# A fused two-block transformer kernel: overlapping row steps with the last attention units, and narrowing the pooling products

## The chip, the cores and the metric

The kernel runs on one core of a Trainium2 chip. The metric is the time of one execution on the device in microseconds (us). Three runs of the kernel before took 3562.31, 3562.95 and 3566.51 us; the median is 3562.95 us.

## The reference

Everything is in fp32. A first block runs twice (layers 0 and 1) over 256 tokens of `x` and 256 tokens of `ctx`, each 2048 wide; a second block (retention, recurrence, cross attention, feed-forward) follows once and is not touched. What concerns us in a layer:

```
p  = h @ w_in[l]                       # pool values, pool gate, q, k, v, attention gate
q, k = rope(rms_norm(q)), rope(rms_norm(k))    # per 64-wide half head; ctx rows have no rope
# 8 heads, each of two 64-wide halves:
a  = softmax(q0 @ k0.T) - lam * softmax(q1 @ k1.T)
o  = rms_norm(a @ v)                   # per head of 128
pooled = windowed mean over tokens (2, 4, 8 or 16 wide) - v   # four groups of 256 columns
x  = x + gate * (concat(mix(pooled) * silu(pool gate), o * silu(attention gate)) @ w_out[l])
```

In layer 0 the queries of both `x` and `ctx` are served (x queries see all 512 keys, ctx queries the 256 of ctx); in layer 1 only those of `x`. The windowed mean is a product with a constant 256 x 256 matrix per window size, which is zero away from a band round its diagonal: no token looks further than 8 tokens back or ahead.

## The kernel before

**Products.** Every large product streams its weights in pieces of 256 rows by 512 columns. ScalarE rounds a piece to `w_hi` (`split_hi`), VectorE makes the remainder `w_lo` (`split_lo`), and TensorE adds three fp32r products, hi by hi, lo by hi and hi by lo, for two groups of 128 rows and each token tile of 128 (`piece_pe`, L617 on). A piece is thus 24 matmuls for four token tiles and 12 for two. `w_hi` and `w_lo` are rings of four; the splits are made three pieces ahead (`AHEAD`). A chunk is eight pieces. At its end ScalarE copies the result to `stage` (`store_act`) and POOL's queue stores it to DRAM (`store_pool`). For four tiles ScalarE takes those copies in the chunk's last piece, ahead of whatever else is woven in there, and so is held until that piece ends.

**What is woven in.** Each engine has its own instruction stream, written as a generator of steps. `together` runs the pieces of a list of products and, after each piece, takes as many steps of the woven generator as the rate says (`advance`). With a rate of 1.125 every eighth piece is followed by two steps; with 1.25 every fourth; with 0.75 three steps fall on four pieces. All engines use the same rates, so step s stands after the same piece on each of them. Nothing but semaphores ties them together: VectorE and ScalarE may run up to three pieces ahead of TensorE.

**The attention stage.** In each layer it is woven into 64 pieces (`beside0`, `beside1`). In layer 0 all have four token tiles; in layer 1 the first 16 pieces have four and the other 48 have two. The stage handles four heads at a time (a group, `attn[l][hg]`, hg = 0, 1). A group has, in this order:

- 2 empty steps (time for loads);
- 7 row steps. Four tiles of q and k rows, numbered k, are normalised and turned. For tiles 0 and 1 one step squares (ScalarE), sums (VectorE), takes the root (ScalarE) and scales (VectorE); a second applies rope (six VectorE instructions, L1060 to L1064). Tiles 2 and 3 have one step each. TensorE transposes the tiles (L1115) in row steps 2, 4, 5 and 6, and ScalarE copies the results to `qT`, `kT`;
- 16 units in layer 0 and 8 in layer 1, plus 2 draining steps. In step s TensorE makes the scores of unit s (L1130), transposes the probabilities of unit s - 1 (L1138) and multiplies those of unit s - 2 with v (L1146). Between them VectorE takes the maximum (L1073), ScalarE the exponential (L1002), VectorE the combination (L1084), ScalarE the copies (L1010, L1016);
- closings, 2 in layer 0 and 1 in layer 1: the rms norm of the results (square L1023, sum L1089, root L1025, scale L1093) and their store to `o1`.

After group 1 comes `close_*`, 14 steps in layer 0 and 20 in layer 1: pooling (`pooling_pe`), mixing, gating, turning. In all that is 29 + 29 + 14 = 72 steps in layer 0 (rate 1.125) and 20 + 20 + 20 = 60 in layer 1 (rate 1.25 for 16 pieces, 0.75 for 32, 1.0 for 16).

`rt` holds the squares of even row tiles and of the closings; `e_sb[:, 0]` those of odd row tiles; both halves of `e_sb` hold exponentials of units. Row tile 2 is loaded into `aT`, which the units also use.

**Pooling.** For each of 8 column blocks `pooling_pe` adds two fp32 products over the 256 output tokens: one over source tokens 0 to 127 and one over 128 to 255. It runs three times in the kernel: x and ctx of layer 0, x of layer 1. A full fp32 matmul stands as two records in the trace.

Of the kernel before, what the change touches and what calls it, by code (L numbers as in the profile page):

```python
# [9 lines left out]
ALU = mybir.AluOpType  # L10
ACT = mybir.ActivationFunctionType
AX = mybir.AxisListType

P = 128
# [63 lines left out]
def build_program(nc, t, out):  # L78
    ctx = ExitStack()
    with ctx:  # L80
# [834 lines left out]

        inv_q = small[:, 160:192]
        squares = [rt, e_sb[:, 0].rearrange("p x c -> p (x c)")]

        def group_pool(pool, gr, l, hg, rows_ready, v_ready, following):
# [6 lines left out]
            for tt in range(4):  # L926
                pool.dma_start(v_sb[:, tt, :], p1[tt, :, O_V + 512 * hg:O_V + 512 * hg + 512]).then_inc(v_loaded, 16)
            yield
            yield
            slots, turned = slots_of(gr)  # L930
            for n in range(len(slots) + 1):
                if turned.get(n) == 0:
                    load_qk(pool, gr, hg, 3)
                yield
            for s in range(len(gr["units"]) + 2):
                if following and s == len(gr["units"]) - 2:
                    wait_all(pool, following[1])
                    load_qk(pool, following[0], hg + 1, 0)
                    load_qk(pool, following[0], hg + 1, 1)
                if not following and s == 1:  # L940

                    pool.wait_ge(qk_T, 2 * gr["m0"] + 8)
                    pool.dma_start(poolA[:], t["pool_a"]).then_inc(pl_a_loaded, 16)
                yield
            if not following:

                pool.wait_ge(o_ready, gr["n0"] + len(gr["units"]))
                wait_all(pool, stored_by(plan[f"beside{l}"][-5]))
                pooling_pool(pool, 2 * l, l, [0, 1])
                pool_weights(pool, l)  # L950
            for c in range(gr["closings"]):
                pool.wait_ge(on_done, gr["c0"] + c + 1)
                for tt in (2 * c, 2 * c + 1):
                    pool.dma_start(o1[tt, :, 512 * hg:512 * hg + 512], o_tok[:, tt, :]).then_inc(o_stored, 16)
                yield

        def group_act(act, gr):
            yield
            yield
# [58 lines left out]
            for c in range(gr["closings"]):  # L1018
                act.wait_ge(o_copied, gr["n0"] + len(units))
                if gr["c0"] + c:  # L1020
                    act.wait_ge(on_ssq, gr["c0"] + c)
                act.wait_ge(qk_done, gr["m0"] + 4)
                nc.scalar.activation(rt[:], o_tok[:, 2 * c:2 * c + 2, :].rearrange("p t c -> p (t c)"), ACT.Square).then_inc(on_sq, 1)  # L1023
                act.wait_ge(on_ssq, gr["c0"] + c + 1)
                nc.scalar.activation(small[:, 136:144], small[:, 128:136], ACT.Sqrt, bias=eps_col[:], scale=1.0 / P).then_inc(on_rms, 1)  # L1025
                yield

        def group_dve(dve, link, gr):
            yield
            yield  # L1030
            slots, turned = slots_of(gr)
            for s in range(len(slots) + 1):
                if s < len(slots):
# [52 lines left out]
                yield  # L1086
            for c in range(gr["closings"]):
                dve.wait_ge(on_sq, gr["c0"] + c + 1)
                nc.vector.tensor_reduce(small[:, 128:136], rt[:].rearrange("p (h c) -> p h c", c=P), AX.X, ALU.add).then_inc(on_ssq, 1)  # L1089
# [4 lines left out]
                yield  # L1094

        def group_pe(pe, gr):
            yield
            yield
# [1413 lines left out]
        for l in range(DEPTH):  # L2512
            groups = []
            for hg in range(2):
                preps = [(tt, l == 0 or tt < XT) for tt in range(4)]
                units_ = [(h, qt, 0 if qt < XT else 2, 4 if qt < XT else 2) for h in range(4) for qt in range(4 if l == 0 else 2)]
                gr = dict(ada=(10, 12)[l], preps=preps, units=units_, m0=m, n0=n, c0=c0, closings=2 if l == 0 else 1, loads=[], evacs=[])
# [11 lines left out]
                groups.append(gr)  # L2529
            attn.append(groups)  # L2530

        def attention_pool(pool, l):
            for hg, gr in enumerate(attn[l]):
                first = plan["lanes0"][2] if l == 0 else plan["lanes1"][1]
                beside = plan[f"beside{l}"]
                rows_ready = [(ada_used, KT * (10, 12)[l])] + stored_by(first)
                following = None if hg else (attn[l][1], stored_by(beside[1 - l]))
                steps = group_pool(pool, gr, l, hg, rows_ready, stored_by(beside[l]) if hg else [], following)
                for n, _ in enumerate(steps):
                    if hg == 0 and n == 1:  # L2540
                        gate_rows_pool(pool, l)
                    if hg == 0 and n == 11:
                        gate_keep_pool(pool, l)
                    yield
            yield from close_pool(pool, l)

        def attention_act(act, l):
            for gr in attn[l]:
                yield from group_act(act, gr)
            yield from close_act(act, l)  # L2550

        def attention_dve(dve, link, l):
            for hg, gr in enumerate(attn[l]):
                for n, _ in enumerate(group_dve(dve, link, gr)):
                    if hg == 0 and n == 10:
                        gate_rows_dve(dve, link, l)
                    yield
            yield from close_dve(dve, link, l)

        def attention_pe(pe, l):  # L2560
            for gr in attn[l]:
                yield from group_pe(pe, gr)
            yield from close_pe(pe, l)

        ATTN_RATE = [1.125, [1.25] * 2 + [0.75] * 4 + [1.0] * 2]

        block = ctx.enter_context(nc.Block())

# [356 lines left out]
```

## Time and profile before

| what | value |
|---|---|
| runs | 3562.31, 3562.95, 3566.51 us |
| the profiled execution | 3565.26 us |
| its span in the trace | 3563.6 us |
| TensorE busy | 3495.1 us (98%), granted clock 0.996 on average |
| VectorE, ScalarE, POOL busy | 1893.7, 1650.5, 220.2 us |
| attention stage of layer 0 | about 476 to 935 us of the span |
| attention stage of layer 1 | about 1296 to 1560 us |

The profiled execution is 1.7 us longer than its span. TensorE is busy nearly always, but a busy TensorE isn't one at its peak: its clock can be granted at half, and a record's end is modelled. The rows further down say where it waits and what it waits for. A granted clock of 1.00 is 2.4 GHz and 0.50 is 1.2 GHz.

### The profile page before, as it was taken

Reading aid. Unit: us, or ns where it says so; the run is one execution under the profiler, and the core shown is the slowest. Engines: PE = TensorE matmul, PEld = TensorE weight load, DVE = VectorE, ACT = ScalarE, POOL = GpSimd, SP = SyncE. Lnnn points to the kernel's source line nnn. Section 1 sums busy time; section 2 is a strip of 40 time slices with the busy share of each in tenths; the row PEclk is TensorE's granted clock in tenths of the full one; section 3 lists DMA queues with packets and bytes.
Section 4 is the critical chain, followed back from the end, with each engine's and each line's share of the span. In section 5 each row is a group of like instructions: output and inputs, shape, how many; then the busy total and the mean of one; then the engine's idle time right before and its main releaser. Section 6 shows DMA issues by size and latency. Waiting matters only on the chain.

```text
span 3563.6 us, 45550 instructions
## 1 busy us (share of the span) xinstructions
PE 3495.1 (98%) x17098; PEld 2820.0 (79%) x17098; DVE 1893.7 (53%) x2345; ACT 1650.5 (46%) x2157; POOL 220.2 (6%) x409
## 2 busy tenths in 40 slices
PE   7999999999999999999999999999999999999998
PEld 5777777777888777688888888888888888888887
DVE  3361134543477335656547775566644566666544
ACT  5441234444345234544545654444454466666433
POOL 2010010101000011000010000000000000000000
PEclk9999999999999999999999999999999999999999
DMA  9979952424566753576777667676654666666665
GB/s 361 345 265 352 331 169 94 142 89 152 194 210 210 242 192 132 172 234 186 217 241 227 212 212 261 204 239 189 208 171 149 188 185 186 183 186 185 201 194 160
DMA packets 331250, 736.85 MB, mean 207 GB/s; under 512 B 26359, under 2 KB 26961, under 8 KB 327872
## 3 DMA queue, kind: packets, MB, share of 16 engines
q1 hardware_dynamic: 300224, 627.12, 55.3%
q0 software_dynamic: 30704, 106.24, 8.4%
q8 instruction: 119, 1.95, 0.2%
q10 hardware_dynamic: 144, 1.05, 0.1%
q14 instruction: 59, 0.48, 0.0%
HBM read 689.10 MB, written 45.21 MB: 206 GB/s over the span
## 4 chain that ended last, share of the span: by engine, by line
PE 93%; DVE 4%; ACT 2%; DMA 1%; issue 1%; POOL 0%; ACTq 0%; SPq 0%; DVEq 0%; POOLq 0%
PE psum L624 28%; PE psum L626 27%; PE psum L625 27%; PE psum L493 2%; DVE w_lo L526 1%; PE psum L1130 1%; PE psum L1146 1%; ACT w_hi L518 1%; PE psum L1173 1%; PE psum L1188 1%; PE psum L2306 1%; PE psum L1138 1%; PE psum L1948 0%; PE psum L686 0%; PE psum L2103 0%
## 5 line engine op out<-in xcount | busy, mean ns | idle before, releaser
L526 DVE TENSOR_TENSOR w_lo<-w_raw,w_hi 128x1024 fp32r<-128x1024 f32 x997 | 1218.6, 1224 | 1424.4 <-ACT w_hi L518 1421.9
L518 ACT ACTIVATE w_hi<-w_raw 128x1024 fp32r<-128x1024 f32 x997 | 1052.9, 1059 | 1369.6 <-PE psum L626 1307.4
L624 PE MATMUL psum<-w_hi,a_hi 128*128 128x512 f32 x3072 | 1219.3, 397 | 4.5 <-DVE a_lo L1230 1.9
L626 PE MATMUL psum<-w_hi,a_lo 128*128 128x512 f32 x3072 | 1198.4, 390 | 0.0
L625 PE MATMUL psum<-w_lo,a_hi 128*128 128x512 f32 x3072 | 1197.2, 390 | 0.0
L624 PEld LDWEIGHTS psum<-w_hi,a_hi 128*128 128x128 f32 x3072 | 578.0, 188 | 137.2 <-issue 12.6
L626 PEld LDWEIGHTS psum<-w_hi,a_lo 128*128 128x128 f32 x3072 | 577.4, 188 | 122.5
L625 PEld LDWEIGHTS psum<-w_lo,a_hi 128*128 128x128 f32 x3072 | 578.3, 188 | 115.3
L624 PE MATMUL psum<-w_hi,f_hi 128*128 128x512 f32 x704 | 276.0, 392 | 0.0
L626 PE MATMUL psum<-w_hi,f_lo 128*128 128x512 f32 x704 | 274.2, 390 | 0.0
L625 PE MATMUL psum<-w_lo,f_hi 128*128 128x512 f32 x704 | 273.9, 389 | 0.0
L562 POOL DMA_DIRECT2D p<-stage x152 | 83.1, 548 | 1465.2 <-ACT stage L554 760.2
L626 PEld LDWEIGHTS psum<-w_hi,f_lo 128*128 128x128 f32 x704 | 132.2, 188 | 27.8
L625 PEld LDWEIGHTS psum<-w_lo,f_hi 128*128 128x128 f32 x704 | 132.3, 188 | 26.7
L624 PEld LDWEIGHTS psum<-w_hi,f_hi 128*128 128x128 f32 x704 | 132.2, 188 | 26.7
L1002 ACT ACTIVATE e_sb<-psum,small 128x512 f32<-128x512 f32 (+1 forms) x96 | 67.0, 702 | 181.3 <-DVE small L1074 181.2
L624 PE MATMUL psum<-w_hi,g_hi 128*128 128x512 f32 x352 | 137.1, 390 | 0.0
L626 PE MATMUL psum<-w_hi,g_lo 128*128 128x512 f32 x352 | 137.0, 389 | 0.0
L625 PE MATMUL psum<-w_lo,g_hi 128*128 128x512 f32 x352 | 136.9, 389 | 0.0
L624 PE MATMUL psum<-w_hi,mem_hi 128*128 128x512 f32 x256 | 102.7, 401 | 3.0 <-DVE mem_lo L2616 3.0
L625 PE MATMUL psum<-w_lo,mem_hi 128*128 128x512 f32 x256 | 100.5, 393 | 0.0
L626 PE MATMUL psum<-w_hi,mem_lo 128*128 128x512 f32 x256 | 100.5, 392 | 0.0
(384 smaller groups left out, 2783.7 us busy)
## 6 DMA issues: line engine op xcount, KB each, us to landing
w_raw<-w_in SPq DMA_DIRECT2D x416, 512.0 KB, 4.3
ada_raw<-w_ada SPq DMA_DIRECT2D x192, 512.0 KB, 7.1
w_raw<-ffn_w_up SPq DMA_DIRECT2D x176, 512.0 KB, 3.7
w_raw<-w_out SPq DMA_DIRECT2D x96, 512.0 KB, 4.7
w_raw<-ffn_w_down SPq DMA_DIRECT2D x88, 512.0 KB, 4.7
p<-stage POOLq DMA_DIRECT2D x152, 256.0 KB, 4.5
w_raw<-xa_w_k SPq DMA_DIRECT2D x32, 512.0 KB, 8.9
w_raw<-xa_w_v SPq DMA_DIRECT2D x32, 512.0 KB, 6.3
```

The source lines that it names most:

```text
L493: mm = nc.tensor.matmul(psum[32 * j:32 * j + 2, ADA_BANK[u % 2], 0:256], cond_st[:, kt, :], ada_raw[ada_home[a]][:, j, :], start=kt == 0, ...
L518: nc.scalar.activation(w_hi[:, slot], raw_of(k), ACT.Copy).then_inc(hi_ready, 1)
L526: nc.vector.tensor_tensor(w_lo[:, slot], raw_of(k), w_hi[:, slot].bitcast(F32), ALU.subtract).then_inc(lo_ready, 1)
L562: pool.dma_start(g.more["to"](tt, g.col(i, c, g.body)), stage_of(g, c, tt)).then_inc(stored[bank], 16)
L624: nc.tensor.matmul(acc, g.hi[:, tt, kt, :], w_hi[:, slot, kk, :], start=first, stop=False)
L625: nc.tensor.matmul(acc, g.hi[:, tt, kt, :], w_lo[:, slot, kk, :], start=False, stop=False)
L626: mm = nc.tensor.matmul(acc, g.lo[:, tt, kt, :], w_hi[:, slot, kk, :], start=False, stop=last)
L1002: nc.scalar.activation(e_sb[:, n % 2, x, 0:nk * P], psum[:, 4 + x, 0:nk * P], ACT.Exp, bias=small[:, sm + x:sm + x + 1], scale=inv_q[:, 8 ...
L1130: nc.tensor.matmul(psum[:, 4 + x, 0:nk * P], qT[64 * x:64 * x + 64, h, qt * P:(qt + 1) * P], kT[64 * x:64 * x + 64, h, k0 * P:(k0 + nk) * ...
L1138: mm = nc.tensor.transpose(psum[:, 6, b * P:(b + 1) * P], a_sb[:, (n - 1) % 2, b * P:(b + 1) * P], ident[:])
L1146: mm = nc.tensor.matmul(psum[:, 7, 0:P], aT[:, n % 2, b * P:(b + 1) * P], v_sb[:, k0 + b, h * P:(h + 1) * P], start=b == 0, stop=b == nk - 1)
L1173: mm = nc.tensor.matmul(psum[:, b, 256 * (cc % 2):256 * (cc % 2) + 256], pv[:, m, cc * P:(cc + 1) * P], poolA[:, cc // 2, m, :], start=m = ...
```

## The change

Four things change together.

1. The steps of a layer are laid out by `staggered`. The second group has no empty steps, and starts when the first has its two draining steps and its closings still before it, so that in those steps both parts are executed, the first's part ahead of the second's on each engine. `close_*` likewise starts with the second group's closings. Layer 0 now has 64 steps (second group from step 25, close from step 50) and layer 1 has 54 (17 and 34).
2. The rates become 1.0 in layer 0, and 1.0, 0.6875 and 1.0 in layer 1.
3. Buffers and loads are adapted: the closings square into `e_sb[:, 1]` (with two added waits on ScalarE), the second group's tiles 0 and 1 are loaded two unit steps earlier, its tile 2 and its v move to the row step in which tile 3 was loaded already.
4. The pooling product over source tokens 128 to 255 is made for output tokens 120 to 255 alone (136 columns in place of 256).

```diff
         def group_pool(pool, gr, l, hg, rows_ready, v_ready, following):
+            def values():
+                wait_all(pool, v_ready)
+                for tt in range(4):
+                    pool.dma_start(v_sb[:, tt, :], p1[tt, :, O_V + 512 * hg:O_V + 512 * hg + 512]).then_inc(v_loaded, 16)
+
             if hg == 0:
                 wait_all(pool, rows_ready)
-                load_qk(pool, gr, hg, 0)
-                load_qk(pool, gr, hg, 1)
-            load_qk(pool, gr, hg, 2)
-            wait_all(pool, v_ready)
...
-            yield
-            yield
+                for k in range(3):
+                    load_qk(pool, gr, hg, k)
+                values()
+            for _ in range(gr["idle"]):
+                yield
             slots, turned = slots_of(gr)
             for n in range(len(slots) + 1):
                 if turned.get(n) == 0:
+                    if hg:
+                        load_qk(pool, gr, hg, 2)
                     load_qk(pool, gr, hg, 3)
+                    if hg:
+                        values()
                 yield
             for s in range(len(gr["units"]) + 2):
-                if following and s == len(gr["units"]) - 2:
+                if following and s == len(gr["units"]) - 4:
...
         def group_act(act, gr):
...
+                    if s == 1 and gr["c0"]:
+                        act.wait_ge(on_ssq, gr["c0"])
...
-                act.wait_ge(qk_done, gr["m0"] + 4)
-                nc.scalar.activation(rt[:], o_tok[:, 2 * c:2 * c + 2, :].rearrange("p t c -> p (t c)"), ACT.Square).then_inc(on_sq, 1)
+                act.wait_ge(a_ready, gr["n0"] + len(units))
+                nc.scalar.activation(o_squares, o_tok[:, 2 * c:2 * c + 2, :].rearrange("p t c -> p (t c)"), ACT.Square).then_inc(on_sq, 1)
...
         def pooling_pe(pe, s):
...
-                for m in range(XT):
-                    mm = nc.tensor.matmul(psum[:, b, 256 * (cc % 2):256 * (cc % 2) + 256], pv[:, m, cc * P:(cc + 1) * P],
-                                          poolA[:, cc // 2, m, :], start=m == 0, stop=m == XT - 1)
+                for m, first in ((0, 0), (1, P - 8)):
+                    mm = nc.tensor.matmul(psum[:, b, 256 * (cc % 2) + first:256 * (cc % 2) + 256], pv[:, m, cc * P:(cc + 1) * P],
+                                          poolA[:, cc // 2, m, first:], start=m == 0, stop=m == XT - 1)
...
+        def staggered(l, first, second, closing):
+
+            units = len(attn[l][0]["units"])
+            second_at = attn[l][0]["idle"] + 7 + units
+            going = [(0, first), (second_at, second), (second_at + 7 + units + 2, closing)]
+            step = 0
+            while going:
+                for part in list(going):
+                    if part[0] <= step:
+                        try:
+                            next(part[1])
+                        except StopIteration:
+                            going.remove(part)
+                step += 1
+                if going:
+                    yield
...
-        ATTN_RATE = [1.125, [1.25] * 2 + [0.75] * 4 + [1.0] * 2]
+        ATTN_RATE = [1.0, [1.0] * 2 + [0.6875] * 4 + [1.0] * 2]
```

## Rows read from the trace of the kernel before

**Rows 1.** The page: the chain that ended last, by engine.

```profile
PE 93%; DVE 4%; ACT 2%; DMA 1%; issue 1%; POOL 0%; ACTq 0%; SPq 0%; DVEq 0%; POOLq 0%
```

**Rows 2.** Waits of TensorE, layer 0's stage (480 to 930): total us, times, longest.

```profile
PE psum L1130 <- ACT e_sb L1002: 5.6, 3, 2.5
PE psum L1115 <- DVE qk L1054: 4.9, 1, 4.9
PE psum L1115 <- DVE qk L1064: 1.4, 1, 1.4
PE psum L1138 <- DVE a_sb L1084: 0.8, 2, 0.5
PE psum L1146 <- ACT o_tok L1016: 0.6, 1, 0.6
```

**Rows 3.** Stretches of TensorE: length, busy us (instructions), granted clock, DMA share, GB/s.

```profile
530.00:535.00 5.00, 5.00 (x17) 0.67 0.21 52
...
760.00:765.00 5.00, 4.65 (x19) 0.50 0.00 0
...
825.00:830.00 5.00, 3.27 (x15) 0.68 0.45 177
...
1365.00:1370.00 5.00, 3.27 (x21) 1.00 0.35 105
```

**Rows 4.** The chain that ended last, in order of time: start, us, what.

```profile
527.80 1.97 PE psum L1115 x8
...
552.06 0.89 PE psum L1146 x8
...
761.75 1.71 PE psum L1146 x8
...
874.79 6.91 PE psum L1173 x32
```

**Rows 5.** Waits of TensorE, layer 1, the sixteen four-tile pieces (1296 to 1401).

```profile
PE psum L1130 <- ACT e_sb L1002: 1.7, 1, 1.7
PE psum L1115 <- DVE qk L1064: 1.0, 1, 1.0
PE psum L1130 <- ACT kT L989: 0.7, 1, 0.7
PE psum L1138 <- DVE a_sb L1084: 0.4, 1, 0.4
```

**Rows 6.** Waits of TensorE, layer 1, the two-tile pieces (1401 to 1500).

```profile
PE psum L1138 <- DVE a_sb L1084: 2.7, 5, 1.1
PE psum L1115 <- DVE qk L1064: 2.0, 2, 1.4
PE psum L1115 <- DVE aT L1054: 1.1, 1, 1.1
PE psum L1130 <- ACT e_sb L1002: 1.0, 2, 0.7
PE psum L1115 <- DVE qk L1054: 0.7, 1, 0.7
```

**Rows 7.** VectorE's timeline, layer 0, group 0's closing, then group 1's first row tile.

```profile
655.56 1.21 DVE L1089 TENSOR_REDUCE small<-rt 128x8 f32<-128x1024 f32 x1
...
657.38 1.22 DVE L1093 TENSOR_TENSOR o_tok<-o_tok,small 128x1024 f32<-128x1024 f32 x1
...
676.09 1.23 DVE L526 TENSOR_TENSOR w_lo<-w_raw,w_hi 128x1024 fp32r<-128x1024 f32 x1 [4.21 <-ACT w_hi L518]
677.24 1.21 DVE L1044 TENSOR_REDUCE small<-rt 128x16 f32<-128x1024 f32 x1
...
679.31 0.69 DVE L1052 TENSOR_TENSOR qk<-qk,small 128x512 f32<-128x512 f32 x1
...
682.75 1.43 DVE L1060 TENSOR_TENSOR rt<-qk,rope_s 128x256 f32<-128x256 f32 x4
...
685.47 1.23 DVE L1064 TENSOR_TENSOR qk<-qk,rt 128x1024 f32<-128x1024 f32 x1
```

More of the change, by code:

```diff
@@ L917, in build_program @@
         squares = [rt, e_sb[:, 0].rearrange("p x c -> p (x c)")]
+        o_squares = e_sb[:, 1].rearrange("p x c -> p (x c)")
         def group_pool(pool, gr, l, hg, rows_ready, v_ready, following):
+            def values():
+                wait_all(pool, v_ready)
+                for tt in range(4):
+                    pool.dma_start(v_sb[:, tt, :], p1[tt, :, O_V + 512 * hg:O_V + 512 * hg + 512]).then_inc(v_loaded, 16)
             if hg == 0:
                 wait_all(pool, rows_ready)
-                load_qk(pool, gr, hg, 0)
-                load_qk(pool, gr, hg, 1)
-            load_qk(pool, gr, hg, 2)
-            wait_all(pool, v_ready)
-            for tt in range(4):
-                pool.dma_start(v_sb[:, tt, :], p1[tt, :, O_V + 512 * hg:O_V + 512 * hg + 512]).then_inc(v_loaded, 16)
-            yield
-            yield
+                for k in range(3):
[3 more added lines that the diff above has]
+                yield
             slots, turned = slots_of(gr)
@@ L957, in group_act @@
         def group_act(act, gr):
-            yield
-            yield
+            for _ in range(gr["idle"]):
+                yield
             slots, turned = slots_of(gr)
@@ L1028, in group_dve @@
         def group_dve(dve, link, gr):
-            yield
-            yield
+            for _ in range(gr["idle"]):
+                yield
             slots, turned = slots_of(gr)
@@ L1088, in group_dve @@
                 dve.wait_ge(on_sq, gr["c0"] + c + 1)
-                nc.vector.tensor_reduce(small[:, 128:136], rt[:].rearrange("p (h c) -> p h c", c=P), AX.X, ALU.add).then_inc(on_ssq, 1)
+                nc.vector.tensor_reduce(small[:, 128:136], o_squares.rearrange("p (h c) -> p h c", c=P), AX.X, ALU.add).then_inc(on_ssq, 1)
                 dve.wait_ge(on_rms, gr["c0"] + c + 1)
@@ L1096, in group_pe @@
         def group_pe(pe, gr):
-            yield
-            yield
+            for _ in range(gr["idle"]):
+                yield
             slots, turned = slots_of(gr)
@@ L2516, in build_program @@
                 units_ = [(h, qt, 0 if qt < XT else 2, 4 if qt < XT else 2) for h in range(4) for qt in range(4 if l == 0 else 2)]
-                gr = dict(ada=(10, 12)[l], preps=preps, units=units_, m0=m, n0=n, c0=c0, closings=2 if l == 0 else 1, loads=[], evacs=[])
+                gr = dict(ada=(10, 12)[l], idle=0 if hg else 2, preps=preps, units=units_, m0=m, n0=n, c0=c0, closings=2 if l == 0 else 1, loads=[], evacs=[])
                 for k, (tt, has_q) in enumerate(preps):
@@ L2530, in build_program @@
             attn.append(groups)
-        def attention_pool(pool, l):
[L2533 to L2545, printed above, removed]
+        def staggered(l, first, second, closing):
[12 more added lines that the diff above has]
+                if going:
+                    yield
@@ new lines, in first_pool @@
+        def first_pool(pool, l):
+            first = plan["lanes0"][2] if l == 0 else plan["lanes1"][1]
+            rows_ready = [(ada_used, KT * (10, 12)[l])] + stored_by(first)
+            following = (attn[l][1], stored_by(plan[f"beside{l}"][1 - l]))
+            for n, _ in enumerate(group_pool(pool, attn[l][0], l, 0, rows_ready, [], following)):
+                if n == 1:
+                    gate_rows_pool(pool, l)
+                if n == 11:
+                    gate_keep_pool(pool, l)
+                yield
@@ L2547, in attention_act, with first_dve @@
+        def first_dve(dve, link, l):
+            for n, _ in enumerate(group_dve(dve, link, attn[l][0])):
+                if n == 10:
+                    gate_rows_dve(dve, link, l)
+                yield
+        def attention_pool(pool, l):
+            second = group_pool(pool, attn[l][1], l, 1, [], stored_by(plan[f"beside{l}"][l]), None)
+            return staggered(l, first_pool(pool, l), second, close_pool(pool, l))
         def attention_act(act, l):
-            for gr in attn[l]:
-                yield from group_act(act, gr)
@@ L2550, in attention_act @@
-            yield from close_act(act, l)
+            return staggered(l, group_act(act, attn[l][0]), group_act(act, attn[l][1]), close_act(act, l))
         def attention_dve(dve, link, l):
[L2553 to L2558, printed above, removed]
+            return staggered(l, first_dve(dve, link, l), group_dve(dve, link, attn[l][1]), close_dve(dve, link, l))
@@ L2560, in attention_pe @@
         def attention_pe(pe, l):
-            for gr in attn[l]:
-                yield from group_pe(pe, gr)
-            yield from close_pe(pe, l)
-        ATTN_RATE = [1.125, [1.25] * 2 + [0.75] * 4 + [1.0] * 2]
+            return staggered(l, group_pe(pe, attn[l][0]), group_pe(pe, attn[l][1]), close_pe(pe, l))
+        ATTN_RATE = [1.0, [1.0] * 2 + [0.6875] * 4 + [1.0] * 2]
         block = ctx.enter_context(nc.Block())
```

## The prediction

> **What bounds the kernel now.** I read the page's chain first: TensorE carries 93% of it [rows 1]. So only two things shorten the kernel: less work on TensorE, or fewer moments in which it waits or runs at half clock. Then I read TensorE's waits, the view that says who made it wait, over the two attention stages alone, since the change touches nothing else. Layer 0's stage has 5.6 + 4.9 + 1.4 + 0.8 + 0.6 = 13.3 us of them in eight instances [rows 2]. Layer 1's has 1.7 + 1.0 + 0.7 + 0.4 = 3.8 us in the sixteen four-tile pieces [rows 5] and 2.7 + 2.0 + 1.1 + 1.0 + 0.7 = 7.5 us in the two-tile pieces [rows 6]. Last the view of stretches, for the clock: the 5 us after the 4.9 us wait are granted 0.67, those round the 2.5 us wait 0.50, those round another wait for the exponential 0.68, while the stretch with layer 1's 1.7 us wait has 1.00 [rows 3]. The reader is to see that a long wait is paid twice.
>
> **Where the waits of layer 0 come from.** With 1.125 steps per piece, pieces 7, 15, 23, ... take two steps. TensorE then meets step s + 1 right behind step s, with no piece between that hides the hand-over from TensorE to VectorE to ScalarE and back. The 4.9 us wait (row tile 2's transposes followed at once by tile 3's, which VectorE hasn't scaled), the three for the exponential, the 1.4 us one for rope: all belong to such pairs.
>
> **Layer 0, removed.** At one step per piece no pair is left. Each hand-over gets a piece: VectorE's timeline shows its length, from one split to the next 4.21 idle + 1.23 busy = 5.44 us [rows 7]. The 4.9 us wait was shorter than that, so it should vanish, and so should the rest: -13.3 us. The clock returns too. After the first wait eight transposes took 1.97 us, where eight products of equal width take 0.89 at full clock [rows 4]: 1.1 us; then 5 us at 0.67 lose 5 x 0.33 = 1.65 us. The second event loses 5 x 0.50 = 2.5, less 0.35 of waiting counted elsewhere: 2.1 to 2.3 us (its eight value products took 1.71 for 0.89). In the third, 5 x 0.32 = 1.6 us includes idle time, and I take 1.1. Sum 6.1 us. Layer 0 gives back 19.4 us.
>
> **Layer 0, added.** Steps 25 to 28 now hold the first group's drain and both closings beside the second group's first two row tiles. No unit is left there, so TensorE has little to do besides its pieces; VectorE has much. A closing costs VectorE, with its wait for the root, 655.56 to 657.38 + 1.22: 3.04 us. A tile's first row step costs 677.24 to 679.31 + 0.69: 2.76 us; its rope step 682.75 to 685.47 + 1.23: 3.95 us; a split 1.2 us [rows 7]. I count from TensorE's last but one value product of the first group (step 25), because ScalarE's copy of it stands in its queue ahead of the square of row tile 0. 1.4 us later VectorE starts. Up to the end of rope on tile 1 it executes 2 first steps, 2 rope steps, 2 closings and 3 splits: 5.5 + 7.9 + 6.1 + 3.6 = 23.1 us, and I add 1.4 us for two hand-overs with ScalarE (a table load by the root, the qT and kT copies ahead of a split). 1.4 + 23.1 + 1.4 = 25.9 us. TensorE in that time executes four pieces of 5.44 us, one value product group and one set of transposes: 23.1 us. It then wants tile 1's transposes: a wait of 2.8 us. The w ring has three pieces in hand and doesn't run dry; tile 2 (4.1 us of VectorE by the same arithmetic: 2.76 + two more scalings of 0.69) is caught up with. A 2.5 us wait lowered the clock [rows 3], so I add 2 us. Below this, the wait could be 0 (hand-overs all covered and the product set later); above, the 4.9 us of the worst row wait [rows 2] with its 2.75 us of clock, 7.7 us. I take 4.8 us.
>
> **Layer 1, four-tile pieces.** Same reasoning: the pairs go, -3.8 us [rows 5], with no clock in it.
>
> **Layer 1, two-tile pieces.** A piece is 2.72 us here. The rate falls from 0.75 to 0.6875, but the last unit, the drain and the closing of group 0, which stood in the four-tile pieces, now fall into these. Of the eight hand-overs between units five have one piece between them before and five after (I laid out both sequences of steps), so the 2.7 + 1.0 = 3.7 us of unit waits [rows 6] stay. The rows' waits, 2.0 + 1.1 + 0.7 = 3.8 us before, are replaced. The last unit's step is followed after one piece by the drain: 0.6 us, of the size of the five such waits. From ScalarE's copy in the drain step VectorE starts 1.3 us later and must do 2 first steps, 2 rope steps, the closing and, now, 5 splits: 5.5 + 7.9 + 3.0 + 6.0 = 22.4, plus 1.5 of hand-overs: 25.2 us to the end of rope on tile 1. TensorE does six pieces (16.3), a value group and a set of transposes: 18.1 us. The difference of 7.1 us is waited for in two parts, some 1.5 at tile 0's transposes and 5.5 at tile 1's. New sum 3.7 + 0.6 + 7.1 = 11.4 us against 7.5. A 5.5 us wait lowers the clock: after the 4.9 us one 2.75 us were lost, so 2.5 more. Bounds: 3.8 us of row waits as before (nothing added), and twice what I take, 15 us. Layer 1's two-tile pieces cost 6.4 us more, layer 1 as a whole 2.6 us more.
>
> Clock, by row and by rule: the rows lowered it at 2.5 us of waiting and not at 1.7 [rows 3]. The Trainium skill (TensorE: Matmul & The Clock Gate, section Why this matters for your kernels) states that an idle gap of about 3 us between matmul bursts puts the clock back to the lower level. By that rule layer 0's new 2.8 us wait would cost no clock, and two of the three events above would not have either; the trace disagrees with it, at 2.5 us. The sum by the rule would be 2 us shorter in the added part.
>
> **Pooling.** 32 records of 256 columns take 6.91 us, 0.216 each; eight records of 128 columns take 0.89, 0.111 each [rows 4]. 136 columns would be 0.118. In a call 16 of 32 records shrink: 16 x 0.098 = 1.57 us, three calls 4.7 us. All three stand in stretches in which TensorE never waits, so it counts whole. Its bound is zero, if narrow records didn't issue faster; the 128-column row speaks against that.
>
> **Loads and waits at no cost.** Tile 2 and v move behind the closing's result on POOL's queue; two unit-length pieces or more lie between their issue and their use. Tiles 0 and 1 are asked for earlier, into pieces with room. Stores of `stage` queued behind POOL's waits are needed only a chunk later. ScalarE's added waits (`on_ssq` before the second unit's exponential, `a_ready` before a closing's square) are for work finished pieces earlier; behind them the next w_hi would be late, and with it TensorE. SP's queue is passed by nothing. In close, pooling follows the last unit by four pieces (21.8 us) where it was five, and no wait for its loads stands among TensorE's [rows 2].
>
> **Sum.** -19.4 + 4.8 - 3.8 + 6.4 - 4.7 = -16.7 us. The profiled execution took 3565.26, 2.3 above the median of the runs; off its time that gives 3548.6. Against the median: 3562.95 - 16.7 = 3546.
>
> **The rivals.**
> - *Hidden rows (0.12).* VectorE's queue of splits absorbs the merged steps: layer 0 adds nothing, layer 1 waits as before. -19.4 - 3.8 - 4.7 = -27.9: 3535. For it: three pieces in hand. Against: transposes wait for the row tile itself, which no ring covers.
> - *Costlier rows (0.20).* The merged steps cost twice as much: layer 0 9.6, layer 1 12.8 more. -19.4 + 9.6 - 3.8 + 12.8 - 4.7 = -5.5, up to -10 in between: 3555, by some 2 either way. For it: ScalarE and VectorE hand over four more times in the closings, each in strict order, with the w splits between.
> - *It isn't the pairs (0.11).* In layer 0 each pair also stands at a chunk's end, where ScalarE is held by the four `stage` copies. If these make the waits, about two thirds remain: -6.5 - 4.7 + 4.8 + 2.6, about -4: 3559. Against it: layer 1's 1.0 and 1.7 us waits come in mid-chunk pairs (pieces 3 and 11), and the piece after hides 5.44 us in any case.
> - *Slower (0.05).* The third row tile comes late: its load now stands on POOL behind the closing's scaling, and the square that waits for it stands in ScalarE's queue ahead of later w_hi. Once its landing is later than the three pieces in hand (16 us in layer 0, 8 in layer 1), every further us stops TensorE in each layer. It decides from 8.4 us per layer (16.7 / 2) on; at 13 us each, with clock, the time is about 3575. Against: these loads are small and were never waited for.
>
> **How the numbers follow.** Forecast 0.52, with a range of its own of 3541 to 3551. 0.2% is 7.1 us, about what a measurement of this kernel can tell from no change: faster means under 3555.8. Faster: 0.52 + 0.12 + 0.14 of the costlier rows + 0.04 of the third = 0.82. Same: 0.06 + 0.07 = 0.13. Slower 0.05. The range of 3535 to 3556 leaves out half of the hidden rows, the upper tail of the costlier ones, and the rest of the last two: about 0.2.
>
> **What would show it.** In layer 0: no wait for the exponential, no row wait at the last two tiles, granted clock 1.00 at pieces 7, 39 and 47, and one wait of 2 to 4 us at L1115 for L1064 about four pieces after the first group's last unit. In layer 1: nothing waited for in the four-tile pieces, then 1 to 2 and 4 to 7 us at L1115 for L1064, the clock under 1.00 after the second. Pooling: 5.3 us per call for 6.91. I am wrong if waits for L1002 remain in layer 0, or if the wait at L1115 exceeds 8 us.

## The result and the profile after

The changed kernel took 3543.26 us (median of 3540.44, 3542.38, 3544.13 and 3545.01), the kernel before 3564.23 us beside it: a ratio of 0.994, 95% interval 0.9923 to 0.9957. In microseconds that is 21 less, with 15 to 27 inside the interval. The forecast was 16.7 less, 3546 us.

The two profiled executions lie further apart (3565.26 and 3540.44 us, spans 3563.6 and 3538.8), because the first is among the longer of its kernel and the second the shortest of its own. They serve for where the time went, stage by stage; a second profiled execution of the changed kernel stands with the experiments.

TensorE's waits in layer 0's stage (470 to 920 us) of the changed kernel; the columns are total us, times, longest. They answer to the five rows and 13.3 us of [rows 2]:

```profile
PE psum L624 <- DVE a_lo L1239: 1.9, 1, 1.9
PE psum L1124 <- DVE qk L1073: 1.9, 1, 1.9
```

The first of the two stands behind the stage and was there before. The other is new: TensorE wants the second group's row tile 1 before VectorE has applied rope (L1073 is the last rope instruction, L1064 before). All eight waits at doubled steps are gone.

Layer 1, first 1270 to 1375, where there is none (against 3.8 us in [rows 5]), then 1375 to 1480 us (against [rows 6]):

```profile
PE psum L1124 <- DVE qk L1073: 6.0, 2, 4.7
PE psum L1147 <- DVE a_sb L1093: 2.2, 5, 0.5
PE psum L1139 <- ACT e_sb L1011: 1.0, 2, 0.7
```

That is 9.2 us where it was 11.3 in all. The row waits have moved and grown: 6.0 us in two waits, against 3.8 in four. TensorE's timeline shows them singly, with the wait in brackets; the eight transposes after the long one take 1.97 us, at half clock:

```profile
1394.04 1.09 PE L1124 MATMUL psum<-ident,qk 128*128 128x128 f32 x8 [1.30 <-DVE qk L1073]
...
1408.03 1.97 PE L1124 MATMUL psum<-ident,qk 128*128 128x128 f32 x8 [4.71 <-DVE qk L1073]
```

The clock: stretches of 5 us, with length, TensorE busy, granted clock, DMA share and GB/s. In layer 0 every stretch of this execution has 1.00 (compare [rows 3]); only the long wait of layer 1 is followed by less:

```profile
675.00:680.00 5.00, 3.08 (x18) 1.00 0.96 363
680.00:685.00 5.00, 5.00 (x24) 1.00 0.36 120
...
1405.00:1410.00 5.00, 1.97 (x9) 0.76 0.93 307
1410.00:1415.00 5.00, 5.00 (x21) 0.90 0.72 244
```

The chain in order of time (start, us, what) has the three pooling calls at 5.31 us, 6.91 before [rows 4], and with the wait's row from TensorE's timeline it gives fixed points to measure stages by:

```profile
473.19 3.13 PE psum L493 x56
845.11 5.31 PE psum L1182 x32
942.10 5.31 PE psum L1182 x32
964.49 3.45 PE psum L1197 x16
1503.49 5.31 PE psum L1182 x32
1520.44 3.45 PE psum L1197 x16
```

```profile
916.39 0.51 PE L624 MATMUL psum<-w_hi,a_hi 128*128 128x512 f32 x1 [1.93 <-DVE a_lo L1239]
```

Layer 0's stage, from the start of the x56 row to the L624 row, lasts 916.39 - 473.19 = 443.20 us. In the kernel before it was 463.45 (473.34 to 936.79): 20.25 us less, the first pooling call's 1.6 among them. The second pooling call gives 1.6. Layer 1 is measured between the last mixing products (L1197, L1188 before) of either layer, which in the kernel before are these:

```profile
986.50 3.45 PE psum L1188 x16
1545.38 3.45 PE psum L1188 x16
```

It went from 558.88 to 555.95 us, of which 1.6 are the third pooling call: 1.3 for the steps. With 20.25 + 1.6 + 1.6 + 1.3 = 24.8 us the whole difference of the two spans is placed. The medians differ by 21; the rest is that these two executions lie on opposite sides of theirs.

### The profile page after: what moved, and what is told of

Read it like the earlier page. It is cut to its first block, busy times and chain, and to the rows that moved or that the text cites. A ratio compares the mean times of both kernels' runs of the same rounds, so it can differ in the third digit from the quotient of the medians.

```text
span 3538.8 us, 45550 instructions
## 1 busy us (share of the span) xinstructions
PE 3484.9 (98%) x17098; PEld 2814.5 (80%) x17098; DVE 1893.9 (54%) x2345; ACT 1648.1 (47%) x2157; POOL 219.4 (6%) x409
## 4 chain that ended last, share of the span: by engine, by line
PE 94%; DVE 3%; ACT 1%; DMA 1%; issue 0%; POOL 0%; ACTq 0%; SPq 0%; DVEq 0%; POOLq 0%
PE psum L624 28%; PE psum L626 28%; PE psum L625 28%; PE psum L493 2%; PE psum L1139 1%; PE psum L1155 1%; DVE w_lo L526 1%; PE psum L1147 1%; PE psum L1197 1%; PE psum L2315 1%; PE psum L1182 0%; ACT w_hi L518 0%; PE psum L1957 0%; PE psum L686 0%; PE psum L2125 0%
## 5 line engine op out<-in xcount | busy, mean ns | idle before, releaser
L624 PE MATMUL psum<-w_hi,a_hi 128*128 128x512 f32 x3072 | 1220.1, 397 | 4.4 <-DVE a_lo L1239 1.9
L624 PEld LDWEIGHTS psum<-w_hi,a_hi 128*128 128x128 f32 x3072 | 577.9, 188 | 136.1 <-issue 12.6
L624 PE MATMUL psum<-w_hi,f_hi 128*128 128x512 f32 x704 | 276.3, 393 | 0.0
L624 PEld LDWEIGHTS psum<-w_hi,f_hi 128*128 128x128 f32 x704 | 132.3, 188 | 26.7
L624 PE MATMUL psum<-w_hi,g_hi 128*128 128x512 f32 x352 | 137.3, 390 | 0.0
L624 PE MATMUL psum<-w_hi,mem_hi 128*128 128x512 f32 x256 | 103.2, 403 | 3.0 <-DVE mem_lo L2639 3.0
```

Source lines behind the costliest of these rows:

```text
L624: nc.tensor.matmul(acc, g.hi[:, tt, kt, :], w_hi[:, slot, kk, :], start=first, stop=False)
```

## The experiments

My theory had three parts: in layer 0 the doubled step itself makes the wait; in the merged steps VectorE's queue of row step, closing and splits is what TensorE waits for; pooling is a fixed 1.6 us per call. Times are medians, each with the ratio to the kernel before that ran on the same chip; the first four, the next four and the last four each ran together, each set on a chip of its own. The last column is the stage's length in the one profiled execution of each kernel.

| kernel | us | ratio, 95% interval | layer 0's stage |
|---|---|---|---|
| changed, again | 3542.70 | 0.9936, 0.9922 to 0.9950 | 443.20 |
| rows first | 3539.04 | 0.9927, 0.9914 to 0.9941 | 441.95 |
| slower row steps | 3542.26 | 0.9935, 0.9922 to 0.9949 | 444.78 |
| both | 3536.22 | 0.9918, 0.9905 to 0.9932 | 441.96 |
| narrowed pooling alone | 3563.06 | 0.9997, 0.9988 to 1.0006 | 460.12 |
| pairs in mid-chunk | 3558.00 | 0.9982, 0.9973 to 0.9991 | 455.41 |
| pairs put back | 3557.08 | 0.9980, 0.9971 to 0.9989 | 458.27 |
| layer 0 alone | 3544.71 | 0.9942, 0.9928 to 0.9955 | 443.20 |
| late closings | 3534.76 | 0.9916, 0.9903 to 0.9930 | 441.05 |
| late, rows first | 3533.92 | 0.9912, 0.9897 to 0.9927 | 441.08 |
| late, slower rows | 3534.07 | 0.9913, 0.9900 to 0.9927 | 441.11 |
| late, units spread | 3533.21 | 0.9913, 0.9899 to 0.9926 | 441.07 |

**Changed, again.** The second profiled execution has the same waits as the first, to 0.01 us, and the same stage of 443.20 us, but a span 2.7 us longer, 3541.5. Its clock fell where the first kept it, behind the 1.93 us wait of L624, and fell lower behind the 4.71 us one. The first execution's stretches, then the second's, then the second's fixed points:

```profile
915.00:920.00 5.00, 3.61 (x19) 1.00 0.49 173
```

```profile
915.00:920.00 5.00, 3.54 (x9) 0.69 0.41 162
...
1410.00:1415.00 5.00, 5.00 (x17) 0.50 0.93 356
```

```profile
943.74 5.31 PE psum L1182 x32
966.12 3.45 PE psum L1197 x16
1523.26 3.45 PE psum L1197 x16
```

From the L624 row (916.46 here) to the second pooling call it takes 27.28 us where the first took 25.71, so 1.6 us are lost there; layer 1 takes 557.14 us where the first took 555.95, 1.2 us more. So the 1.3 us that layer 1's steps gained in the first pair of traces are 0.1 in this one: the gain in layer 1 is no larger than what the clock does from one execution to the next.

**Pairs in mid-chunk.** The kernel before, with `start` handed to `together` for the attention stage:

```
-        def together(product, eng, gemms, woven, rate, flush=True):
-            start = 0.0
+        def together(product, eng, gemms, woven, rate, flush=True, start=0.0):
...
-                together(..., attention_pe(pe, l), ATTN_RATE[l])          # and so on each engine
+                together(..., attention_pe(pe, l), ATTN_RATE[l], start=(0.5, 0.0)[l])
```

> The kernel before with layer 0's doubled steps moved by half a chunk: they fall on pieces 3, 11, 19, ... of the stage, in which ScalarE makes no stage copies, in place of 7, 15, 23, ... Rates, steps and buffers are as before. My theory (the pair itself makes the wait): there are again some six to eight waits, for other steps of the sequence; those of unit pairs 1 to 2.5 us each, the sum 7 to 13 us, the time within 6 us of before. Rival (the pair waits because ScalarE is held by the chunk's stage copies): nearly all waits vanish, the stage shortens by 13 to 19 us, and the time falls by as much.

TensorE's waits in layer 0's stage of this kernel, 9.4 us in eight instances:

```profile
PE psum L1129 <- ACT e_sb L1001: 6.8, 4, 2.6
PE psum L1137 <- DVE a_sb L1083: 1.6, 3, 0.7
PE psum L1114 <- DVE qk L1063: 1.0, 1, 1.0
```

The stage is 8.0 us shorter than before, 4.0 of it in waits and the rest in clock: it is lowered after one wait here instead of three. A pair makes a wait off the chunk's end too. But the chunk's end is no trifle. In the kernel before, ScalarE's timeline ahead of the 4.9 us wait shows tile 3's square directly behind the fourth `stage` copy, which itself waited for the piece's last products:

```profile
518.09 0.60 ACT L552 ACTIVATE stage<-psum 128x512 f32<-128x512 f32 x1
...
522.07 0.60 ACT L552 ACTIVATE stage<-psum 128x512 f32<-128x512 f32 x1 [0.77 <-PE psum L626]
522.56 1.05 ACT L976 ACTIVATE e_sb<-qk 128x1024 f32<-128x1024 f32 x1
```

The four copies stand ahead of that square from 518.09 to 522.56, 4.5 us, about the size of the wait. How much of the 8.0 us is the copies' and how much is that other steps now meet in pairs (the row pair here is tile 0's rope and its transposes, not tiles 2 and 3) is not separated. My bound of 6 us on the time was just missed, at 6.5.

**Pairs put back.** The changed kernel with

```
-        ATTN_RATE = [1.0, [1.0] * 2 + [0.6875] * 4 + [1.0] * 2]
+        ATTN_RATE = [[1.125] * 4 + [0.875] * 4, [1.0] * 2 + [0.6875] * 4 + [1.0] * 2]
```

> The changed kernel with doubled steps again in the first half of layer 0's stage (rate 1.125 for four chunks, 0.875 for the other four); the merged layout, buffers and pooling stay. Doubled steps at pieces 7, 15, 23 and 31. My theory (one step per piece is what gains): the 4.9 us wait and its lowered clock return at piece 7, and waits of 1 to 2.5 us at pieces 15 and 31; layer 0's stage is 9 to 14 us longer than in the changed kernel. Rival (the gain is from the merging of the groups' ends, fewer steps in all): within 3 us of the changed kernel.

Layer 0's stage is 458.27 - 443.20 = 15.1 us longer, a little more than expected, the time 14.4 (the kernels ran on different occasions). Two of its waits, in TensorE's timeline:

```profile
527.99 1.84 PE L1124 MATMUL psum<-ident,qk 128*128 128x128 f32 x8 [4.89 <-DVE qk L1063]
...
675.13 1.97 PE L1124 MATMUL psum<-ident,qk 128*128 128x128 f32 x8 [3.79 <-DVE qk L1073]
```

The first is back as it was. The second is the changed kernel's 1.9 us wait, grown; tile 0's transposes, which did not wait there, wait 1.53 us here. A pair in the merged steps takes one piece of 5.4 us from VectorE's time before these transposes, and 3.4 us of it come back as waiting. Both waits shown were followed by a clock under 1.00. So the rate gains in layer 0, and the merging only makes the lower rate possible (64 steps for 64 pieces).

**Narrowed pooling alone.** The kernel before, with the last hunk of the diff in `pooling_pe` and nothing else.

> The kernel before with the narrowed pooling products alone. My theory: each of the three calls of L1173 takes 5.3 us in place of 6.9, nothing else moves, so the time falls by 4.7 to 4.8 us (0.13%), and all waits of TensorE stay as in the kernel before (13.3 us in layer 0's stage, 11.3 in layer 1's). Rival (the narrowing is eaten by a wait behind it, of ScalarE's copies or of the mixing): the calls shrink but the mixing products start no earlier, and the time stays within 1 us.

The first mixing product behind each call starts 1.6 us sooner after the call's start, so the mechanism is as expected. But the time fell by 1.4 us, not 4.7, and the interval reaches from 2.1 us of loss to 4.3 us of gain: it holds 0, and the expected 4.7 lies just outside. Its profiled execution shows what blurs it. These are 5 us stretches behind the unchanged 1.93 us wait at 933.5 and the unchanged 1.73 us wait at 1366:

```profile
935.00:940.00 5.00, 5.00 (x23) 0.74 0.46 161
...
1365.00:1370.00 5.00, 3.44 (x15) 0.76 0.01 3
1370.00:1375.00 5.00, 5.00 (x22) 0.90 0.08 11
```

In the kernel before the same waits left the clock at 1.00, the second by [rows 3], the first by this:

```profile
935.00:940.00 5.00, 3.21 (x16) 1.00 0.43 167
```

The other way round, behind the 4.90 us wait that both have, the stretch from 530 us is granted 0.86 here and 0.67 before. Which waits near 2 us lower the clock, and how much a longer one costs, changes from execution to execution, and this kernel's eleven runs spread from 3559.2 to 3565.9 us, more than its gain. The 4.8 us are shown in the chain's rows, not in the time; by the time alone the rival (within 1 us) fits as well.

**Layer 0 alone.** The changed kernel with layer 1's steps in sequence:

```
-        ATTN_RATE = [1.0, [1.0] * 2 + [0.6875] * 4 + [1.0] * 2]
+        ATTN_RATE = [1.0, [1.25] * 2 + [0.75] * 4 + [1.0] * 2]
...
-idle=0 if hg else 2
+idle=0 if hg and l == 0 else 2
...
+            if l:
+                going = [(0, first), (20, second), (40, closing)]
```

> The changed kernel with layer 1's attention steps one group after the other again and with the rates before (1.25, 0.75, 1.0); layer 0, the pooling and the loads inside a group stay changed. My theory by the two traces: layer 1's part of the change is worth little, 1 to 2 us in all, since 3.8 us of waits in the four-tile pieces went and the two-tile pieces gained 1.3 + 4.7 us row waits for 3.8; layer 1's stage is 1 to 3 us longer than in the changed kernel, with waits of about 11 us. My prediction's own sizes (layer 1 costs 2.6 us) would make this kernel 2 to 3 us faster than the changed one. Rival (layer 1 gains much through its loads and clock): 5 us or more slower.

It is 2.0 us slower than the changed kernel's second measurement, within what I gave layer 1 by the two traces, and on the other side from my prediction. The two ran on different chips, though, and their intervals overlap, so the time doesn't show it. The waits of layer 1 are 11.3 us, as before, and two of them (1.73 and 2.70 us) lowered the clock in this execution. Between the fixed points layer 1 takes 560.21 us, against 555.95 and 557.14 in the two executions of the changed kernel, and 557.3 in the kernel before with the pooling's 1.6 us taken off. The last has layer 1's steps in the same order and the same sum of waits, so most of those 2.9 us are probably clock. Layer 1's steps gain something from 0.1 to 4.3 us; more isn't shown.

**Rows first.** In `staggered`:

```
-                for part in list(going):
+                for part in reversed(list(going)):
```

> The changed kernel with the merged steps in the other order on every engine: the second group's row step ahead of the first group's drain and closing. My theory (the closing's 3.0 us of VectorE and its root stand ahead of the rows that TensorE waits for): layer 0's 1.9 us wait vanishes; layer 1's 1.3 + 4.7 us shrink by 3 to 4 us, the second below 2.5 us and without a lowered clock; the time is 5 to 8 us below the changed kernel. Rival (VectorE's rope, the splits and the short pieces make the wait, and order is indifferent): layer 1's waits sum to 5 us or more and the time is within 2 us of the changed kernel.

The time fell by 3.7 us, short of the 5 expected, and half of my theory was wrong. Layer 0's wait vanished, with one of 0.7 us at tile 2 in its place, and tile 0's in layer 1 went to 0.2, while tile 1's stayed. TensorE's row, then VectorE's timeline ahead of it:

```profile
1406.11 1.38 PE L1124 MATMUL psum<-ident,qk 128*128 128x128 f32 x8 [4.70 <-DVE qk L1073]
```

```profile
1395.20 0.69 DVE L1061 TENSOR_TENSOR qk<-qk,small 128x512 f32<-128x512 f32 x1
1396.87 1.22 DVE L1098 TENSOR_REDUCE small<-e_sb 128x8 f32<-128x1024 f32 x1 [0.99 <-ACT e_sb L1032]
...
1398.70 1.23 DVE L1102 TENSOR_TENSOR o_tok<-o_tok,small 128x1024 f32<-128x1024 f32 x1
1399.84 2.35 DVE L526 TENSOR_TENSOR w_lo<-w_raw,w_hi 128x1024 fp32r<-128x1024 f32 x2
1402.11 1.42 DVE L1069 TENSOR_TENSOR e_sb<-qk,rope_s 128x256 f32<-128x256 f32 x4
```

Tile 1 is scaled by 1395.9, and its rope (L1069) starts at 1402.1. In between stand the closing (L1098 to L1102, with 0.99 us of waiting for its square) and two splits. For this wait the order within the step doesn't matter, since the rope belongs to the next step, and the closing is ahead of that in either order.

**Slower row steps, and both.** The changed kernel, and rows first, with

```
-[0.6875] * 4
+[0.5] + [0.75] * 3
```

> The changed kernel with layer 1's 22 steps of the first four two-tile chunks dealt as 4, 6, 6, 6 in place of 5.5 each (rates 0.5, 0.75, 0.75, 0.75). Between the drain step and tile 1's transposes there are then seven pieces in place of six. My theory (VectorE's work in that stretch against TensorE's pieces): the two row waits, 6.0 us in the changed kernel, fall by one piece, 2.7 us, and the unit waits stay at 2.7 to 3.7; the time is 2 to 4 us below the changed kernel, the more so where the clock isn't lowered. Rival (units suffer by the tighter dealing behind it): unit waits rise by 2 us or more and nothing is gained.

> Rows first and the slower dealing together. My theory: the row waits of both layers nearly vanish (below 1.5 us in sum), unit waits in layer 1 of 2.5 to 4 us remain; 6 to 10 us below the changed kernel, so 27 to 31 us below the kernel before on the same chip. Rival (both cure the same microseconds): no better than the better of the two alone.

Alone it shows no gain (3542.26 us): tile 0's 1.3 us wait and the 0.5 us one vanish, tile 1's grows from 4.71 to 5.59. The extra piece fell ahead of tile 0's transposes, not between those of tile 0 and 1, where VectorE is short. With rows first it is 6.5 us below the changed kernel, at the low edge of what I expected, though tile 1 still waits 4.07 us. The slower dealing alone also caught the clock. Its instructions in layer 0 are the changed kernel's to the letter, and its wait is 1.91 us where that has 1.92:

```profile
675.00:680.00 5.00, 3.09 (x16) 0.94 0.99 371
680.00:685.00 5.00, 5.00 (x18) 0.72 0.36 108
```

Here the stage lasts 444.78 us, in three other executions of the same code 443.20 each: 1.6 us for a lowered clock after a wait of 1.9.

**Late closings.** Four empty steps ahead of the first group's closings:

```
+            for _ in range(gr["late"]):       # in group_pool, group_act, group_dve, group_pe
+                yield
             for c in range(gr["closings"]):
...
-idle=0 if hg else 2,
+idle=0 if hg else 2, late=0 if hg else 4,
```

> The changed kernel with the first group's closings four steps later in each layer, after the second group's row steps (four empty steps ahead of them in the first group, on every engine). My theory (VectorE's 3.0 us closing between row tile 1's first step and its rope is what TensorE waits out): layer 0's 1.9 us wait vanishes, layer 1's 4.7 us wait falls to 0.5 to 2 us, no lowered clock there, the 1.3 us one stays; the time is 5 to 8 us below the changed kernel. Rival (the splits and the short pieces make the wait, as the order of row and closing within a step did not cure it): the wait stays above 3.5 us.

This is the test of the VectorE theory, and it holds: the first group's results aren't needed for many steps, so its closing can stand behind the rows. Layer 0 has no wait left in its stage, and the stage is 2.15 us shorter, 443.20 to 441.05. In layer 1, TensorE's timeline and the clock round the second wait:

```profile
1391.96 1.09 PE L1130 MATMUL psum<-ident,qk 128*128 128x128 f32 x8 [1.31 <-DVE qk L1077]
...
1403.00 1.09 PE L1130 MATMUL psum<-ident,qk 128*128 128x128 f32 x8 [1.75 <-DVE qk L1077]
```

```profile
1400.00:1405.00 5.00, 3.25 (x19) 1.00 0.85 307
```

4.71 became 1.75 us, by the closing's 3.0 us [rows 7], and the clock stayed. The time is 3534.76 us, 0.9916 of before where the changed kernel has 0.9936. The two ran on different chips and the intervals overlap by a little, but the runs lie apart: 3533.7 to 3535.5 us against 3541.4 to 3543.7, with medians of the kernel before of 3564.9 and 3565.5 beside them. The edit moves ScalarE's square and root of the closing along with VectorE's part, so how the 3.0 us divide between the two engines isn't tested.

**Late closings with rows first, and two dealings of steps.** On top of both edits, rates `[0.5] + [0.75] * 3` for `late_slow`, and `[0.75] + [0.5] * 3` with 1.25 for the last two chunks in `late_spread`.

> Late closings and, in merged steps, the second group's row step ahead of the first group's drain. Rows first alone took the 1.3 us wait to 0.2 and started VectorE 2.5 us earlier, but the closing still stood ahead of the rope. My theory: both row waits of layer 1 below 0.5 us in sum, 1 to 3 us better than late closings alone. Rival: the same as late closings alone, within 0.5 us.

> Late closings, rows first, and layer 1's steps dealt 4, 6, 6, 6 over the first four two-tile chunks. My theory: nothing is left for the slower dealing to cure, so it is within 1 us of the kernel without it, with unit waits of 2.5 to 3 us. Rival (a piece more between row steps is worth what it was beside the closing): 2 us or more better.

> Late closings, rows first, and layer 1's steps dealt 6, 4, 4, 4 over the first four two-tile chunks and 10, 10 over the last two (rates 0.75, 0.5, 1.25), so that units have two pieces between them and the closing stage's steps come faster. My theory: the 2.7 us of unit waits (one piece of 2.7 us between two units doesn't hide their hand-over) vanish, and the closing stage stays hidden: 2 to 3 us below the kernel with late closings and rows first. Rival (doubled steps in the closing stage bring waits for pooling, mixing or turning): new waits of 2 us or more at its lines and no gain.

The three lie within 0.9 us of each other and 1.6 of late closings alone; none can be told from another by time. So the 1 to 3 us that I expected of rows first, and the 2 to 3 of spreading the units, did not come; only the slower dealing did as I said. The traces show why. Rows first cures tile 0's wait (0.20) and leaves tile 1's (1.75), where I had expected both under 0.5 in sum. The slower dealing leaves two unit waits of six, but one of them is 2.12 us long and lowers the clock. Spreading the units removes all unit waits, as expected, but packs the row steps, and tile 1 waits longer:

```profile
1400.88 1.32 PE L1130 MATMUL psum<-ident,qk 128*128 128x128 f32 x8 [3.77 <-DVE qk L1077]
```

No wait appeared in its closing stage. The best kernels measured are the four with late closings, 0.9912 to 0.9916 of before, some 31 us. But rows first with the slower dealing, which leaves the closing where it was, has 0.9918, and the intervals don't tell it from them: its waits in the two stages (without the L624 one) sum to 6.8 us, those of late closings alone to 6.3, those of the changed kernel to 11.1. Two edits together there do what one does here.

## Why the prediction was right

The time lay 3 us under the forecast, inside the range. Against the kernel before that ran beside it, the gain was 21.0 us for 16.7 forecast. Step by step, by the first two profiled executions, which lie 24.8 us apart:

| step | forecast | measured |
|---|---|---|
| layer 0, waits at pairs | -13.3 | -13.3 |
| layer 0, clock (what is left over) | -6.1 | -7.3 |
| layer 0, merged steps: wait and its clock | +2.8 + 2.0 | +1.9 + 0 |
| layer 1, four-tile pieces | -3.8 | -3.8 |
| layer 1, two-tile pieces: waits | +3.9 | +1.7 |
| layer 1, clock (what is left over) | +2.5 | +0.8 |
| pooling, three calls | -4.7 | -4.8 |

The misses add up to 8.1 us, all on one side, so none made up for another: the costs of the merged steps were put 6.8 us too high in all, the clock that layer 0 gets back 1.2 us too low, the pooling 0.1. That the time is only 3 us off is in part luck: the median that the forecast was taken from lay 1.3 us under the one measured beside the changed kernel, and the two profiled executions lie further apart than the medians.

- *Pairs.* Right in place and size, and tested from both sides: moving the pairs keeps two thirds of the waits, putting four of them back into the changed kernel costs 15.1 us. The third rival (it isn't the pairs) gave 3559 us and waits that remain, and is refuted by the changed kernel, where none do. It was right in that a chunk's end makes a pair worse: with the pairs off it the stage was 8.0 us shorter, in part perhaps because other steps met.
- *The clock.* 7.3 us is what remains of 20.25 after 11.4 of waits and 1.6 of pooling; I had 6.1 by adding up stretches. Gaps too short to be listed are in it as well, and I haven't separated these. The size is also that of one execution: with narrowed pooling alone the stage has the same waits and is 460.12 us long, 1.7 us less than the pooling explains.
- *Merged steps, layer 0.* One wait, at the transposes that I named, for rope. I forecast 2.8 us from 25.9 of VectorE against 23.1 of TensorE, and named 2 to 4 us as the sign; it is 1.9, just under. I charged its clock with 2 us: the changed kernel kept 1.00 there in both its profiles, but the same code lost 1.6 us in the slower-rows run. So the term takes 0 in some executions and 1.6 us in others.
- *Merged steps, layer 1.* 1.5 and 5.5 us were forecast, 1.30 and 4.71 measured. VectorE's timeline of the changed kernel bears out the account, from the closing over tile 1's first step and two splits to its rope:

```profile
1395.04 1.21 DVE L1098 TENSOR_REDUCE small<-e_sb 128x8 f32<-128x1024 f32 x1
...
1396.85 1.23 DVE L1102 TENSOR_TENSOR o_tok<-o_tok,small 128x1024 f32<-128x1024 f32 x1
1398.00 1.22 DVE L1053 TENSOR_REDUCE small<-e_sb 128x16 f32<-128x1024 f32 x1
...
1401.76 2.36 DVE L526 TENSOR_TENSOR w_lo<-w_raw,w_hi 128x1024 fp32r<-128x1024 f32 x2 [0.99 <-ACT w_hi L518]
1404.03 1.42 DVE L1069 TENSOR_TENSOR e_sb<-qk,rope_s 128x256 f32<-128x256 f32 x4
...
1406.75 1.22 DVE L1073 TENSOR_TENSOR qk<-qk,e_sb 128x1024 f32<-128x1024 f32 x1
```

  I was 1 us too high in unit waits (3.7, measured 2.7): I counted pairs of units with one piece between as equal, but one wait of 0.44 us is gone and the last, 1.1 us before, is 0.5 now. The row waits were 1 us too high as well, 7.1 for 6.0. With the clock this made the sign for layer 1 wrong: forecast were 2.6 us lost, measured are 1.3 gained in the first profiled execution and 0.1 in the second, where the clock's part is +2.0, near the 2.5 forecast.
- *Slower row tile 2* (the rival on the other side) did not occur: in layer 1 its load was issued at 1399.4 us and landed 3.4 us later, and ScalarE squared it at 1404.4 without a listed wait.
- *The clock's rule.* The prediction read from its rows that 2.5 us of waiting lower the clock and 1.7 don't. No such line holds. In the kernel before, the third lowered stretch already stands behind a wait of 2.08 us; 1.91 us did in one execution, and 1.73 and 1.93 in another, while 1.92 and 1.93 did not in the changed kernel's first execution, nor 2.39 with pairs in mid-chunk (619.04 us, its stretches all at 1.00). The Trainium skill (TensorE: Matmul & The Clock Gate, section Why this matters for your kernels) names idle gaps of about 3 us as what lowers the clock. The runs disagree on the size, by the same waits.

## What to carry to other kernels

When steps are woven between pieces of a saturated engine, deal them so that no two follow each other without a piece: a doubled step made TensorE wait for up to 4.9 us here, and cost clock besides, most of all where a helper engine was held by other work at that point. When two parts are merged to make room for that, add up the other engines' instructions in program order between two points that TensorE needs, and move whatever isn't needed soon (here a closing) behind both; reordering within a step did nothing for the wait one step later. A gain of a few microseconds is read from fixed points in the trace, as the time of a whole run moves by more; and from two executions, as the clock moves the fixed points too.

## What the runs showed of the hardware that I had not expected

The same instructions after the same wait run at 2.4 GHz in one execution and at 1.2 GHz for some microseconds in the next. It was seen with waits of 1.73, 1.91 and 1.93 us, and cost 1.6 us where it could be measured by itself: 443.20 against 444.78 us for the stage, and 25.71 against 27.28 us behind the L624 wait in two executions of the changed kernel. Of the other waits near 2 us in the two stages, those of 2.08 (the kernel before, 826.26 us) and 2.12 us (late closings with rows first and the slower dealing) lowered the clock; one of 2.07 and one of 2.39 us, both with pairs in mid-chunk, did not. After every wait of 2.5 us and more in the two stages, of all the kernels profiled, it fell, but not by the same amount: after the same 4.90 us wait one 5 us stretch was granted 0.67 in one execution and 0.86 in another.

Such events are one reason for the spread of a kernel's times: the 2.7 us between the changed kernel's two profiled executions are two of them. Whether fewer waits near 2 us narrow the spread isn't shown. The kernel before ranged from 3561.8 to 3567.4 us in 27 runs and the four with late closings from 3532.3 to 3535.5 in 19, but pairs in mid-chunk, with waits of 2.39 and 2.62 us, only from 3557.2 to 3559.2 in 10.
